# Own-key blocks of 128 for the near heads, and the first mixer's shifted copies and head norm in another order

## The reference, cut to what matters

```python
proj = t @ w_in
y_a = diff_attention(proj[..., :3 * DIFF_WIDTH], ...)   # 4 heads: softmax minus lam * softmax, times v,
                                                        # then rmsnorm over 128 columns of each head, * subln * 0.8
y_b = conformer_conv(proj[..., 3 * DIFF_WIDTH:], ...)   # u * sigmoid(g), a causal convolution of width 31
                                                        # in each of 512 channels, layernorm, silu
return concatenate([y_a, y_b], -1) @ w_out
```

```python
c_start = clip(col - 8, 0, 64 - 16)
in_win = (col_k >= c_start) & (col_k < c_start + 16)
s_win = q . k * SCALE + where(in_win, rpb[h, dr, dc], -inf)   # 256 own keys, at most 64 of them open
p = softmax(concatenate([s_win, s_ctx]))
```

## Time and profile before

| what | value |
|---|---|
| median of 3 runs (lowest, highest) | 1873.86 us (1871.81, 1874.7) |
| the profiled execution's own time | 1872.61 us |
| its span | 1870.8 us |
| mean granted clock of TensorE | 0.992 |
| PE busy, DVE busy, ACT busy, POOL busy | 97%, 40%, 49%, 74% |
| near steps of x0 and x1 | 1106 to 1154 us and 1527 to 1575 us |
| first mixer, from the input u's turn to its last chunk | about 58 to 156 us |

### The profile page before, as it was taken

One profiled execution on the slowest core, in us unless ns is written; L12 is line 12 of the kernel. 1 busy time (PEld: TensorE's weight loads), 2 busy tenths in 40 slices (PEclk: granted clock), 3 DMA queues, 4 the chain that ended last, 5 costly groups with the idle time before them and its releaser, 6 DMA issues.

```text
span 1870.8 us, 28082 instructions
## 1 busy us (share of the span) xinstructions
PE 1805.9 (97%) x9454; PEld 1442.0 (77%) x9454; DVE 752.4 (40%) x1423; ACT 917.2 (49%) x1421; POOL 1381.2 (74%) x813
## 2 busy tenths in 40 slices
PE   8889999999999999999999999999999999999997
PEld 6657888766788887777888877778888877778886
DVE  3263532384455564353111555451114655451112
ACT  5246444544634454555344545654446546554443
POOL 6427999538788869568888884578887984578884
PEclk9999999999999999999999999999999999999999
DMA  7787566579788745435666453346664553346662
GB/s 240 189 291 233 183 202 194 188 242 310 265 264 265 258 124 183 130 119 183 212 197 191 151 166 100 102 150 216 201 189 154 162 176 99 104 148 190 191 188 71
DMA packets 253586, 347.17 MB, mean 186 GB/s; under 512 B 20664, under 2 KB 152888, under 8 KB 253496
## 3 DMA queue, kind: packets, MB, share of 16 engines
q1 hardware_dynamic: 250000, 338.23, 56.7%
q10 hardware_dynamic: 3496, 7.78, 1.4%
HBM read 344.29 MB, written 1.64 MB: 185 GB/s over the span
## 4 chain that ended last, share of the span: by engine, by line
PE 87%; DVE 6%; ACT 3%; DMA 2%; POOL 1%; issue 1%; SPq 0%; ACTq 0%; DVEq 0%; POOLq 0%
PE bank L2332 24%; PE bank L2334 24%; PE bank L2333 23%; PE bank L2418 3%; PE bank L2987 2%; PE bank L3014 2%; PE bank L2997 2%; PE bank L2384 1%; DMA raw<-in_l_w_in 1%; ACT wh L810 1%; POOL wl L743 1%; PE bank L2660 1%; POOL wl L742 1%; DMA raw<-in_l_w_uq 0%; DVE X L1497 0%
## 5 line engine op out<-in xcount | busy, mean ns | idle before, releaser
L783 POOL TENSOR_TENSOR wl<-raw,wh 128x1024 fp32r<-128x1024 f32 x300 | 734.2, 2458 | 109.0 <-ACT wh L975 83.3
L2332 PE MATMUL bank<-wh,xh 128*128 128x512 f32 (+2 forms) x1726 | 681.7, 395 | 17.8 <-POOL wl L743 10.3
L2334 PE MATMUL bank<-wl,xh 128*128 128x512 f32 (+2 forms) x1726 | 666.5, 386 | 0.0
L2333 PE MATMUL bank<-wh,xl 128*128 128x512 f32 (+2 forms) x1726 | 664.5, 385 | 0.0
L742 POOL TENSOR_TENSOR wl<-raw,wh 128x512 fp32r<-128x512 f32 (+2 forms) x234 | 317.4, 1356 | 320.0 <-ACT wh L810 319.9
L975 ACT ACTIVATE wh<-raw 128x1024 fp32r<-128x1024 f32 x270 | 286.2, 1061 | 434.3 <-PE bank L2334 422.2
L2332 PEld LDWEIGHTS bank<-wh,xh 128*128 128x128 f32 x1726 | 325.5, 189 | 90.4 <-issue 16.4
L2334 PEld LDWEIGHTS bank<-wl,xh 128*128 128x128 f32 x1726 | 325.2, 188 | 66.9
L2333 PEld LDWEIGHTS bank<-wh,xl 128*128 128x128 f32 x1726 | 326.1, 189 | 60.2
L810 ACT ACTIVATE wh<-raw 128x1024 fp32r<-128x1024 f32 (+2 forms) x268 | 276.2, 1050 | 174.4 <-PE bank L2334 109.4
L743 POOL TENSOR_TENSOR wl<-raw,wh 128x512 fp32r<-128x512 f32 (+2 forms) x234 | 310.2, 1326 | 0.0
(11 more groups left out here) (376 smaller groups left out, 1696.5 us busy)
## 6 DMA issues: line engine op xcount, KB each, us to landing
raw<-in_w_ffn_in SPq DMA_DIRECT2D x264, 256.0 KB, 3.0
raw<-in_w_in SPq DMA_DIRECT2D x224, 256.0 KB, 2.9
raw<-in_w_mod SPq DMA_DIRECT2D x152, 256.0 KB, 4.5
raw<-in_w_ffn_out SPq DMA_DIRECT2D x132, 256.0 KB, 2.8
raw<-in_l_w_gate SPq DMA_DIRECT2D x88, 256.0 KB, 3.7
raw<-in_l_w_up SPq DMA_DIRECT2D x88, 256.0 KB, 4.3
raw<-in_l_w_down SPq DMA_DIRECT2D x88, 256.0 KB, 3.4
raw<-in_l_w_in SPq DMA_DIRECT2D x48, 256.0 KB, 4.6
```

Of the source, the lines that this page charges most:

```text
L783: nc.gpsimd.tensor_tensor(wl[:, s, :], raw[:, s, :], words(wh)[:, s, :], ALU.subtract)\
L2332: mm(dst, x_hi, w_hi, start=first, stop=False, skip_group_check=True)
L2333: mm(dst, x_lo, w_hi, start=False, stop=False, skip_group_check=True)
L2334: return mm(dst, x_hi, w_lo, start=False, stop=last, skip_group_check=True)
```

## The change

Two things at once.

**Near heads.** A group g of 64 queries is now 16 grid columns in 4 rows. The own keys that any of them sees are 32 columns in 4 rows: 128 keys from column 0, 8, 24 or 32 (`WINDOWS`). `q` is written in group order by its turn, and the output is put back in token order by DVE. Own scores of a unit are 2 matmuls of 64x64 queries by 128 keys, into the two halves of the bank's partitions; context scores are 2 matmuls of 64x64 by 256 keys. A unit has 384 keys in place of 512, so that bias, maximum, exponential, turns and copies work on less. For the products with v, the windows' rows are gathered by 16 transfers of 32 partitions into `v_windows`, issued by SP ahead of one chunk of `w_in`; own values are 8 matmuls of 64 moving columns. The bias table has 2048 columns in place of 3072, and the latent stream's v lives in memory of the gates. The context stream and the far heads are as before.

**First mixer.** The 4 transfers to `shifted0` move from ACT to SP, behind all loads of `in0` and ahead of those of `mod0_scores`. `shifted1b` and `shifted1a` move behind the loads of `mod0_scores`. ACT squares the attention's output straight from the bank, DVE sums it, and the scaling reads the bank. On PE the convolution's mean comes ahead of the turn of the attention's output and of `mod0_outputs`; on DVE the mean is subtracted ahead of the splits.

```diff
 # SP
                     if name == "mod0_scores":
+                        sp.wait_ge(u_out[0], 16)
+                        for j in range(4):
+                            sp.dma_start(shifted0[32 * j:...], shift_of(0, j, slice(0, 4))).then_inc(shift_in[0], 16)
+                    if name == "mod0_rows":
                         sp.wait_ge(u_out[1], 16)
                         ... (shifted1b; wait qk_tr 4; shifted1a)
                     for j in range(plan.first[name], plan.end(name)):
+                        if name in ("in_x0", "in_x1") and j == plan.tiles[name][PRELUDE + 2][2][2][0]:
+                            sp.wait_ge(evac, plan.tile_no[name] + PRELUDE)
+                            for g, first_col in enumerate(WINDOWS):
+                                for r in range(4):
+                                    at = 64 * (r % 2) + first_col
+                                    sp.dma_start(v_windows[32 * r:32 * r + 32, g, :], vv[XS][at:at + 32, r // 2, :]).then_inc(v_in, 16)
                         load(j)
 # ACT
             copy_u(1)
-            act.wait_ge(u_out[0], 16)
-            for j in range(4):
-                act.dma_start(shifted0[32 * j:...], shift_of(0, j, slice(0, 4))).then_inc(shift_in[0], 16)
 ...
+            step(nc.scalar.activation(spare, eps6, ACT.Sqrt))
+            for qb in range(2):
+                act.wait_ge(pv_done, qb + 1)
+                nc.scalar.activation((s0, s1)[qb]...[:, 0:DW], bank[2 + qb][:, :], ACT.Square).then_inc(o_square, 1)
             for qb in range(2):
                 act.wait_ge(o_sq, qb + 1)
 # DVE
             for qb in range(2):
-                dve.wait_ge(pv_done, qb + 1)
-                step(v.tensor_copy(o0[:, qb, :], bank[2 + qb][:, :]))
-                settle()
-                step(v.tensor_tensor(sq, o, o, ALU.mult))
-                settle()
+                dve.wait_ge(o_square, qb + 1)
                 v.tensor_reduce(osq[:, 4 * qb:4 * qb + 4], sq, AX_X, ALU.add).then_inc(o_sq, 1)
 ...
-                step(v.tensor_tensor(o, o, spread(rs...), ALU.mult))
+                step(v.tensor_tensor(o, bank[2 + qb]..., spread(rs...), ALU.mult))
 ...
+            dve.wait_ge(conv_mean, 1)
+            v.tensor_tensor(yc, yc, mean, ALU.subtract).then_inc(conv_xc, 1)
             dve.wait_ge(o_tr, 2)
             for pair in range(2):
                 split(2 * pair, 2, bank[4 + pair][:, :], xt_split)
-            dve.wait_ge(conv_mean, 1)
-            v.tensor_tensor(yc, yc, mean, ALU.subtract).then_inc(conv_xc, 1)
             discretise()
 # PE, scores of near heads in x0 and x1
+                def window_scores(i, h, qb):
+                    for own in (True, False):
+                        for gg in range(2):
+                            g = 2 * qb + gg
+                            for e in range(2):
+                                r = slice(64 * e, 64 * e + 64)
+                                b = unit_bank(2 * i + e)[64 * gg:64 * gg + 64]
+                                lhs = qT[r, h, 64 * g:64 * g + 64]
+                                if own:
+                                    keys = kT[XS][r, h, :].rearrange("p (r c) -> p r c", r=4)[:, :, WINDOWS[g]:WINDOWS[g] + 32]
+                                    mm(b[:, 0:P], lhs, keys, ...)
+                                else:
+                                    ins = mm(b[:, P:P + SEQ], lhs, kT[CTX][r, h, :], ...)
 # PE, values of near heads in x0 and x1
+                def window_values(c):
+                    if c == 0:
+                        pe.wait_ge(v_in, 16 * 4 * len(WINDOWS) * (l + 1))
+                    for t in range(TT):
+                        for e in range(2):
+                            mm(bank[6][64 * e:64 * e + 64, 0:SEQ], vv[CTX][:, t, at:at + HD], pT2[:, e, 1 + t, :], ...)
+                    for g in range(len(WINDOWS)):
+                        for e in range(2):
+                            mm(bank[6][64 * e:64 * e + 64, 64 g:64 g + 64], v_windows[:, g, at:at + HD], pT2[:, e, 0, 64 g:64 g + 64], ...)
 # PE, first mixer
-            pe.wait_ge(o_norm, 2)
-            pe.wait_ge(tap_out, 3)
-            turns of o0, modulate("mod0_outputs")
             pe.wait_ge(tap_out, CONV_T)
             normalised(0, yc..., conv_mean)
+            pe.wait_ge(o_norm, 2)
+            turns of o0, modulate("mod0_outputs")
```

More of the change, by code:

```diff
@@ L64, with window_columns @@
 CCOL, NC = columns(CON)
+def window_columns():
+    p, first = np.arange(P), np.array(WINDOWS)
+    group = 2 * np.arange(2)[None, :] + (p // 64)[:, None]
+    return p % 64 // 16, (16 * group + (p % 16)[:, None])[:, :, None], first[group][:, :, None] + np.arange(32)
 def constants():
@@ L417, in build @@
         bias_at = used["b2"]
[L418 removed]
+        bias = view("b2", 2, NAH, 4, 32)
         kT, vv = [None, None], [None, None]
@@ L1354, in half_block @@
                     act.wait_ge(xt_split, split_at[f"m_{name}"] + 4)
-                ffn(f"ffn_{name}", sg2, [lambda h=h: load_bias(("c0", "x0").index(name), slice(h, h + 2)) for h in range(0, NAH, 2)]
+                ffn(f"ffn_{name}", sg2, [lambda part=part: load_bias(("c0", "x0").index(name), part) for part in range(4)]
                     if name != "x1" else [], ahead)
@@ L2188, in top @@
                         if u == 0:
[L2189 to L2191 removed]
+                            dve.wait_ge(bias_set, 2 * l + 2)
+                        own = unit_bank(u)[:, 0:P]
+                        near = bias[:, i % 2, 2 * (i // 2) + e].rearrange("p a b -> p (a b)")
                         step(v.tensor_tensor(own, own, near, ALU.add))
@@ L2707, in _ @@
             normalised(0, yc.rearrange("p a b -> p (a b)"), conv_mean)
+            pe.wait_ge(o_norm, 2)
+            for b in range(2):
+                turn(bank[4 + b], lambda i, t: o0[:, t, (2 * b + i) * P:(2 * b + i + 1) * P], o_tr)
+            modulate("mod0_outputs")
             x_ready("out0", 2)
@@ L2934, in qk_turn @@
                         pe.wait_ge(qt_ev, qt_at[name] + max(b if b >= 5 else b - 1, 0))
-                    turn(qk_banks(name, s)[b][1], src, qt_tr)
+                    turn(qk_banks(name, s)[b][1], src, qt_tr, grouped=s == XS and what == "q")
                 if name == "c1":
@@ L2981, in scores @@
                     q = slice(qb * P, qb * P + P)
+                    if s == XS and near:
+                        window_scores(i, h, qb)
+                        return
                     for n, k in enumerate(sets):
@@ L3007, in values @@
                         tr(bank[6][:, SEQ + qb * P:SEQ + qb * P + P], rspread[:, c % 2, qb * P:qb * P + P], ident)
+                    if s == XS and near:
+                        window_values(c)
+                        return
+                    n_keys = SEQ * len(sets)
                     for n, k in enumerate(sets):
```

88 lines of the change are left out of this document (54 added, 34 removed).

## The result

The changed kernel takes 1856.59 us (median of 6 runs, 1852.87 to 1858.83), the kernel before on the same chip 1873.04 us (6 runs, 1871.72 to 1876.64). The ratio is 0.9908, with a 95% interval of 0.9895 to 0.9921. The forecast was 1855.5 us, in a range of 1850 to 1860. The profiled execution took 1852.87 us, its span is 1851.1 us.

A forecast was written before the change was run, and what follows sets the result against it. PE was taken to bound the kernel (87% of the chain). First mixer 9.7 us plus near heads 8.6 gave 18.3 us, so 1854.3 profiled and 1855.5 as median; forecast's own range 1850 to 1860, whole range 1849 to 1866.5.

The forecast's parts named there:

- (a): First mixer: moving the four `shifted0` issues off ACT and behind the `in0` loads gains 6.0 us, lower end 3.0.
- (b): First mixer: PE's 3.17 us wait before the first `mod0_scores` chunk goes, gaining 3.1 us, lower end 1.5.
- (c): First mixer: squares on ACT and the mean ahead of the turns gain 0.6 us, ends -1.0 and 2.0.
- Turns: Near heads: six turns for eight, 0.216 us less in each of 16 steps, 3.5 us in all, called certain.
- Scores: Near heads: four quarters of the array run side by side, -0.21 us a step, -3.4 us in all.
- D: Near heads: only pairs of quarters overlap, so the near heads lose 3.4 us; 1867.6 us in all; chance 0.06.
- E: Near heads: quarters of the array do not overlap at all, scores +27.6 us; 1888.3 us in all; chance 0.05.
- Values: Near heads: own values as 16 short passes, -0.41 to 0.03 us per pair of steps, taken -0.2, -1.7 in all.
- rival B: Near heads: a floor on short passes (0.054 us a pass), so only the turns gain there; 1860.7 us; chance 0.18.
- DVE: Near heads: DVE saves 0.3 us per unit, and its hole in step 5 stays near 1.0 us.
- v's windows: Near heads: SP's 16 transfers of v's windows stay hidden; if not, 0 to 3 us lateness once per layer.
- Rival C: First mixer: transfers stay in the way and PE waits for `shifted0` or `shifted1a`; mixer gains 4, 1861.3 us; chance 0.12.

The follow-up runs named there:

- c_transfers: Kernel before with only the shifted copies' transfers moved from ACT to SP and behind the loads, norm and order as before: 1863.5 us, ratio 0.9938.
- f_no_norm: Changed kernel with the head norm and PE's order as before, near heads and moved transfers kept: 1853.96 us, ratio 0.9893.
- b_mixer: Kernel before with only the first mixer's half of the change, attention as before: 1864.17 us, ratio 0.9947.
- d_norm: Kernel before with only the head norm's squares on ACT and the mean ahead of the turns, transfers as before: 1876.69 us, ratio 1.001.
- g_again: Second run of the changed kernel with the variance's normalising put ahead of the second chunk of `out0`: 1856.21 us, ratio 0.990.
- k_out_sooner: Changed kernel with the three `w_mod` chunks ahead of `out0` put behind it: 1861.52 us, ratio 0.9937.
- e_ctx_whole: Changed kernel with the near heads' context score products undivided, own keys still on quarters of the array: 1857.64 us, ratio 0.9908.

## Why the prediction was right, and where it was not

The mechanisms of the large terms held and the sum came out: 18.3 us forecast, 19.4 in the stretches, 16.5 and 18.1 in the medians. The stretches gave 10.05 and 9.33 us where 9.7 and 8.6 were forecast. Part of this closeness is luck: in both halves the errors of single terms, up to 2 us, cancel. The low end of the whole range, 1849 us, does not follow from the parts: their good ends, 11 and 10.5 us, give 1852.4.

- *(a) ACT's issues and the DMA share, (b) the wait of 3.17 us.* Right, in what shows it too: rounding at 60.92 (61.5 said), clock 1.00 from 64 to 76, no hole of 2.6 us, none before `mod0_scores`. The two were 9.1 us together in the forecast. `c_transfers`, which has only them, gave 11.38 us between the marks (87.76 against 99.14), where no stretch at half clock came behind its hole of 2.84 us; `f_no_norm`, with the same mixer code and a clock of 0.51 behind that hole, gave 10.44. So the two terms were 1.3 to 2.3 us too small. PE's first scores (L2648, at 89.18 before) split them. Up to there the gain is 5.63 us in `c_transfers`, 5.27 in `f_no_norm` and 5.26 in the changed kernel: (a) was forecast at 6.0 as if both holes closed, and 0.35 and 1.04 us of them are left. From the scores to the turns of o it is 5.06 us less than before in both of these kernels, where (b) had 3.1. Most of what is missing is the clock behind the hole of 3.17 us, which (b) put at nothing though (a) had priced it for the hole of 2.61. A window of the kernel before, right behind that hole:

```profile
96.25:99.65 3.40, 3.40 (x40) 1.83 (x44) 2.34 (x10) 3.00 (x14) 0.00 (x0) 0.59 1.06 388
```

  The same work of PE, from this `w_mod` chunk to the row of 72 passes of the convolution, takes 5.16 us there (96.25 to 101.41) and 3.46 at full clock in `c_transfers` (87.82 to 91.28): 1.70 us. How (a) divides between ACT's issues and the DMA share was not tried; the late roundings above speak for the DMA share.
- *(c) norm and order.* Taken at 0.6, ends -1.0 and 2.0. Measured alone 0.04; on top of the transfers -0.83 (`b_mixer` against `c_transfers`) and about -0.36 (the changed kernel against `f_no_norm`). By the split above it is 10.05 - 5.26 - 5.06 = -0.27. Since the same mixer code differs by 0.94 us between two traces (87.76 and 88.70), all of these say: about nothing. The hole moved to `w_out` as forecast, and the clock fell after it as feared. But what (c) had wrong is the path: it counted 0.7 us for an earlier start of `out0` and 0.5 us for the reciprocal, and only the second is on the path. The reciprocal gained 0.06 us in `d_norm`, as `discretise` became longer and the root came late. In `g_again` the clock behind the hole was full and the stretch was still no shorter. (The old start of `out0` is 129.99 in the trace, not the 130.4 of the prediction.) A term of the sum that was mis-sized, within its range. The cause of the late chunk (a slot that hangs on a `w_mod` chunk) is shown by `k_out_sooner`.
- *Turns.* 0.80 us for six as forecast, 3.5 us in all.
- *Scores.* 0.81 to 0.88 against 0.85 forecast, 3.4 us in all. Four quarters side by side, two by two, do overlap. Rivals D (1.5 us a step) and E (2.8 us) are excluded.
- *Values.* The mis-sized term. Forecast -0.2 us for a pair of steps, 1.7 us in all; measured 1.88 - 1.48 = 0.40, so 3.2. The 16 short passes take 0.47 us, 0.029 us each, below the 0.054 us of the earlier trace rows that rival B took for a floor. In the trace the two passes of a pair start 7 ns apart and the pairs follow each other at 0.058 us. That is the prediction's own 0.056 for two overlapping loads, worked out from the earlier trace rows, and 8 x 0.056 = 0.45 was its good end; what went wrong is that it took a middle value, -0.2, between its two ends. B is excluded by this row. The Trainium skill ("TensorE: Matmul & The Clock Gate", section "Wait — 56ns, not 53.3ns?") puts 62 ns as sequencer time of a matmul with hardware decode off; by that figure the prediction had 0.99 us for these passes, and they take 0.47, but which decoding ran, and how far the sequencer was ahead, no run shows. That section of the Trainium skill also has a least distance of 25 ns from start to start, and from this the trace differs, with its 7 ns between passes on two halves of the array.
- *DVE.* The forecast had the hole in step 5 stay near 1.0 us: 0.65. It had none of the 0.45 us behind DVE's norm and rotation at 1111.17, nor that PE's wait for DVE's copy of v grows from 0.39 to 0.64 us in x0 and x1. DVE's own saving was as said (557 for 691 ns, 291 for 426).
- *v's windows.* Wrong in x1. Priced at nothing with "0 to 3 us each" if the cover failed, and it fails by 0.92 us once (0.90 to 0.96 in eight other traces with this code, 0.50 in `e_ctx_whole`). SP's timeline, first x0, then x1:

```profile
1093.99 10.08 SPq L727 DMA_DIRECT2D arena<-arena  x16
...
1514.07 10.04 SPq L727 DMA_DIRECT2D arena<-arena  x16
```

  SP needs 0.63 us for each of the 16 issues, not the 0.5 of the earlier trace rows. In x0 it begins 2.5 us behind the start of DVE's copy, in x1 5.6 us behind it, since it first has a chunk of `w_in` to issue whose slot comes free only at 1513.2 (POOL's `wl` is the link ahead of it in the chain). It ends at 1524.1, and the last transfer lands at 1525.5.
- *The sum of the near heads.* 3.5 + 3.4 + 3.2 = 10.1 us of PE's work, less some 1.1 us of waits that are longer or new than before, leaves 9.0; measured 9.33. The error of -1.5 in the values and that of +1.1 in the waits nearly cancelled.
- *Rival C* (transfers in the way): excluded; no wait for `shifted0` or `shifted1a` in any of the traces with the change.

## What to carry to other kernels

A transfer that is issued early shares DMA with the weights that PE needs next; moved behind them it cost nothing here and gave 10 to 11 us. Before reordering work for a gain, look for the instruction at a fixed distance from the end of the stage: here DVE's reciprocal, 19.4 us ahead of it, told what a change was worth, and an earlier start of PE's work did not. Ask of each queue what stands at its head when the new work arrives, in every instance of the stage: the same 16 transfers were covered in x0 and late in x1. When a ring of slots feeds PE, chunks moved away from one hole push every later load back, and the bill comes at the next stage (1.8 us ahead, then 6.2 behind).

## What the runs showed of the hardware that was not expected

- Passes of 64 columns with 64 columns of weights, two side by side, run at 0.029 us each (16 in 0.47 us), the two of a pair 7 ns apart.
- Four quarters of the array work off their own passes, whatever the order in which the program mixes them (0.39 and 0.43 us in either order).
- The same context scores cost 0.63 us as 4 passes over halves and 0.43 to 0.50 us as 8 over quarters, when they follow passes over quarters.
- Behind holes of 2.76 to 2.84 us the granted clock sometimes stayed at the upper level (1.00 in `c_transfers` and `g_again`) and sometimes fell to the lower (0.57 in the changed kernel, 0.51 in `f_no_norm`). Same mixer code, with and without: 87.76 and 88.70 us.
- DVE instructions on 128x8 take 0.15 to 0.20 us, or 1.1 to 1.3 us while POOL makes `wl` (five of 15 in the changed kernel's `discretise`, two to three with the order as before). Each long one ends within 0.1 us of a `wl` instruction in the four traces read for it (`before`, `after`, `d_norm`, `g_again`).
